# First stage of a decoder-layer kernel: modulation slabs and sample query strips issued earlier, weight sums moved on VectorE

## The chip, the core and the metric

The program runs on one core of one Trainium2 chip. Its time is the device time of one execution in microseconds, as a median of several runs. The engines are TensorE (PE in the profile, its weight loads PEld), VectorE (DVE), ScalarE (ACT), GpSimd (POOL) and SyncE (SP); each runs its own list of instructions in order, and they wait for one another with counting semaphores. SP and ACT issue the DMA transfers, each on a queue of its own (q1 carries what SP issues, q10 what ACT issues).

## The reference, cut to what matters

One layer for 1024 prompt rows and 8 sample rows (one new token each, with 4096 cached positions in pages of 128). All in float32:

```python
shift, scale, gate = split(silu(c) @ w_ada + b_ada, 3)
h = rmsnorm(x, g_pre) * (1 + scale) + shift
hc, bc, cc, gc, q, k, v, ga = split(h @ w_in, 8)      # 512 columns each
u = cc * hc
ya = rmsnorm(bc * conv3(u), g_conv) * silu(gc)
o = stick_breaking_attention(q, k, v, b_sb)            # sample rows: over the paged cache
yb = rmsnorm(o, g_attn) * silu(ga)
y = x + gate * rmsnorm(concat(ya, yb) @ w_out, g_post)
```

## The kernel before

The kernel has a first stage, then four groups g of two heads and 128 conv channels (SLOTS = 32 slots t of each group), then the output projection. The order on each engine is written out by hand, so every engine's function lists its own steps.

**First stage.** x is scaled and turned into hT (eight slices k of 128 channels, by 1056 columns). `ada(n)` (line 1508) multiplies silu(c) with slab n of w_ada: shift and scale of the lower half of the channels are slabs 0 and 1, of the upper half 2 and 3. ACT copies each result (`ada_copy`, 755), `mod_sums(a)` (1538) adds up its four strips, and DVE's `modulation(a)` (1109), `modulate_samples(a)` (1120) and `modulate(a, c)` (1126) scale and shift the half a of hT, counting up h_ready. `project_qk(m, a)` (1545) is a sixth of group 0's Q and K projection for half a; the halves a = 1 close the sums, and ACT takes them out in `evac_qk` (788).

**Sample queries.** `strips(DB, ..., 4)` (1592) projects the sample rows to all heads' queries; ACT copies them to qsP (769), `query_rows` (1558) adds the strips, ACT copies the rows (771), writes them to q_rows in DRAM (773), waits until that has landed (774) and reads two of them back into qb, broadcast over the partitions (776). GpSimd's page products (673) can start only then: each multiplies one pair of K pages with qb, and DVE's `reduce_pair` (1337) sums each. There are two `prod` buffers, so product p waits for reduction p - 2. SP loads the K pages into a ring of four pairs (474).

**Gates.** `gate_strips(n)` (1513) projects slabs 4 and 5 of w_ada (numbered 5 and 7 as loads), ACT copies them (`gate_strips`, 778), `gate_sums(n)` (1521) adds them on PE, and DVE's `gates(n)` (1151) makes gps and gp in four dependent steps. `gate_strips(1)` waits for three steps of `gates(0)`.

**Group 0's block products.** A projection pair is made with Strassen-like products `product(g, i, j)` (1760): chunk i, product j of seven. Chunks 2 and 3 of group 0 are V and B. Products 3, 5 and 6 read sums of weights, which for V and B DVE makes in four steps (`value_weight_sum`, 1182), with S1 lying in the same tile as qsP; product 7 reads the fourth. `product(0, 2, 4)`, code 24, waits at line 1797 for d_c22, which DVE's `product_sum(.., 2, 7)` (1207, 1227) counts. That sum stands in slot t = 6 of DVE's list, behind the reductions of page pairs 0 to 9 (slots 1 to 5) and before `gates(1)`. EARLY_FIRST (101) is PE's order of codes in slots 6 and 7 of group 0, TAKEN_FIRST (103) ACT's order of taking them out.

**Loads.** `load_w` (783) on ACT loads 512 KB of w_in in rows of 512 bytes. In slot 0 of group 0, V and B are loaded when qk_full reaches 1 (792, 793). SP loads slab 5 of w_ada (line 476) after four K page pairs and once ada_ps has reached 5.

Of the kernel before, what the change touches and what calls it, by code (L numbers as in the profile page):

```python
# [27 lines left out]
ALU = mybir.AluOpType  # L28
# [4 lines left out]
D = 1024  # L33
KT = D // P
SEQ = 1024
TT = SEQ // P
NB = 8
NT = SEQ + NB
NTP = SEQ + 32
# [9 lines left out]
EPS = 1e-6  # L49
# [94 lines left out]
def stick_breaking_mixer(nc, x_prompt, x_sample, c_prompt, c_sample, cache_k, cache_v, state_conv,  # L144
# [4 lines left out]
    with ctx:  # L149
# [564 lines left out]
        def _(act):  # L714
# [52 lines left out]
            ada_copy(3)  # L767
            act.wait_ge(qs_ps, 1)
            run(qsP, ps[:, DB, :], ACT.Copy, qs_copied, scale=HD ** -0.5)
            act.wait_ge(qs_ps, 2)  # L770
            run(qsP[0:NB, :], ps[0:NB, DB, :], ACT.Copy, qs_copied)
            act.wait_ge(qs_copied, 2)
# [15 lines left out]
            def evac_qk(g, m):  # L788

                act.wait_ge(qk_full, m + 1)  # L790
                if m == 0:
                    load_w(g, V_, 2)
                    load_w(g, BC_, 3)
                if m == 2:
                    load_w(g, GC_, 0)
                if m == 5:
                    load_w(g, GA_, 1)
                src = ps[:, QK_BANK[m], :]
                if m < 3:
                    n = CH if m < 2 else SEQ - 2 * CH  # L800
                    run(qT[:, CH * m:CH * m + n], src[:, 0:n], ACT.Copy, qk_free, scale=HD ** -0.5)
                else:
                    run(kT[:, CH * (m - 3):CH * (m - 2)], src[:, 0:CH], ACT.Copy, qk_free)
# [140 lines left out]
            def body(g, first, last):  # L944
                for t in range(SLOTS + 1):
                    u = t - 8
                    if 0 <= u < NU:
                        lo, head = first_col(u), UNITS[u][3]
                        act.wait_ge(zc_ready, NU * g + u + 1)
                        if not (first and u < 2):  # L950
                            act.wait_ge(lw_ready, NU * g + u - 1)
                        run(rise[:, u % 2, lo:QC], ps[:, Z + u % 3, 0:QC - lo], ACT.Relu, rise_ready,
                            bias=bsh[:, bass.ds(2 * g + head, 1)])
                        z = sp[:, lo:QC]
                        if not (first and u < 1):
                            act.wait_ge(ln_done, NU * g + u)
                        run(z, zc[:, u % 3, lo:QC], ACT.Exp, exp_done)
                        act.wait_ge(exp_done, NU * g + u + 1)
                        run(ps[:, Z + u % 3, 0:QC - lo], z, ACT.Ln, ln_done, bias=1.0)
                    if u >= 1:  # L960
                        weights(g, u - 1, first)
                    if first and t < 6:
                        evac_qk(g, t)
                    for code in (TAKEN_FIRST if first else TAKEN).get(t, ()):
                        evac_st(g, code // 10, code % 10)
                    if t in (4, 6) and not first:
                        squares(g - 1, t // 6)
                        if t == 4:
                            sample_columns(g - 1)
                    if t == 7:  # L970
                        value_rows_copy(g, first, 0)
                        key_rows_copy(g, 0, first)
                    if t == 9:
                        value_rows_copy(g, first, 1)
                    if t == 8:
                        key_rows_copy(g, 1, first)
                    if t == 19:
                        out_copy(g)
                    if t >= 8 and t < SLOTS and u % 2 == 1:
                        i = u // 2  # L980
                        for back, j in {0: ((-1, 4), (0, 1)), 1: ((0, 5), (0, 2), (0, 6)), 2: ()}[i % 3]:
                            evac_st(g, 4 + i // 3 + back, j)
                    if first and t in (1, 5):
                        gate_strips(t // 5)
                    if t == 10:
                        key_rows_copy(g, 2, first)
                    if t in (21, 27):
                        silu_step(g, t // 27, 0)
                    if t in (22, 28):
                        silu_step(g, t // 28, 1)  # L990
                    if t in (23, 29):
                        silu_step(g, t // 29, 2)
                    if t in (25, 31):
                        silu_end(g, t // 31)
                    if t == 11:
                        decode_logs(g, 0)
                    if t == 19:
                        decode_a(g, 0, first)

                evac_st(g, CHUNKS - 1, 4)  # L1000
                for j in () if last else AHEAD[:2]:
                    evac_st(g + 1, 0, j)
                decode_logs(g, 1)
                for j in () if last else AHEAD[2:]:
                    evac_st(g + 1, 0, j)
                decode_a(g, 1, first)
# [37 lines left out]
        def _(v):  # L1044
# [51 lines left out]
            for k in range(KT):  # L1096
                v.wait_ge(xT_full, k + 1)
                v.tensor_copy(hT[:, k, 0:HALF], ps[:, k % 4, :]).then_inc(xT_dve, 1)
            v.wait_ge(ssq, TT + 1)
            v.tensor_scalar(ss[:, 4:TT], ss[:, 4:TT], 1.0 / D, EPS, ALU.mult, ALU.add).then_inc(var_ready, 1)  # L1100
            v.tensor_scalar(ss[0:NB, TT:TT + 1], ss[0:NB, TT:TT + 1], 1.0 / D, EPS, ALU.mult, ALU.add)\
                .then_inc(var_ready, 1)
            v.wait_ge(rstd_ready, 3)
            row_scales(4)
            v.tensor_scalar(xs, xs, rs[0:NB, TT:TT + 1], None, ALU.mult).then_inc(x_scaled, 1)
# [123 lines left out]
            def body(g, first, last):  # L1229
# [18 lines left out]
                for t in range(SLOTS):  # L1248
                    u = t - 8
                    if u >= 1:  # L1250
                        log_weights(g, u - 1, first)
                    if t == 18 and g == 2:
                        own_heads(0)
                    if t == 20 and g == 2:
                        own_heads_copy(0)
                    chunk = (SUMMED_FIRST if first else SUMMED).get(t)
                    if u > 0 and u % 6 == 0:
                        chunk = 3 + u // 6
                    if chunk is not None:
                        product_sum(g, first, chunk, 3)  # L1260
                        product_sum(g, first, chunk, 7)
                    if first and t == 6:
                        gates(1)
                    if u >= 0 and u % 2 == 0:
                        clamp(g, u, first)
                        clamp(g, u + 1, first)
                    if t == 14:
                        decode_log_weights(0)
                    for p in sums_at(t):
                        reduce_pair(g, p)  # L1270
                    if t in (2, 3):
                        value_weight_sum(g, 2 * (t - 2))
                        value_weight_sum(g, 2 * (t - 2) + 1)
                    if not first and t in GATING_AT:
                        gating(g - 1, GATING_AT[t])
                    if first and t == 0:
                        channel_sums()
                    if first and t == 0:
                        gates(0)

                log_weights(g, NU - 1, first)
# [197 lines left out]
        def _(pe):  # L1479
# [99 lines left out]
            pe.wait_ge(xT_act, 5)  # L1579
            project_qk(0, 0)  # L1580
            ada(2)
            pe.wait_ge(xT_act, 6)
            project_qk(1, 0)
            ada(3)
            pe.wait_ge(xT_act, 7)
            project_qk(2, 0)
            mod_sums(1)
            pe.wait_ge(ada_copied, 4)
            project_qk(3, 0)
            project_qk(4, 0)  # L1590
            pe.wait_ge(h_ready, 14)
            strips(DB, lambda k: hT[:, k, SEQ:NTP], 4).then_inc(qs_ps, 1)
            project_qk(5, 0)
            query_rows()
            project_qk(0, 1)
            gate_strips(0)
            project_qk(1, 1)
# [1 line left out]
            gate_sums(0)  # L1599
            for m in range(3, 6):  # L1600
                project_qk(m, 1)
            gate_strips(1)

            def body(g, first, last_):
                def value_rows(c):
# [91 lines left out]
                for t in range(8):  # L1697
                    if first and t == 6:
                        pe.wait_ge(qk_free, 6)
                        mm(ps[:, BY, 0:SC], ident[:, :], hT[:, 0, 0:SC], True, True)  # L1700
                    for at, code in enumerate(EARLY_FIRST.get(t, ()) if first else EARLY[t]):
                        product(g, code // 10, code % 10)
                        if first and t == 6 and at == 0:
                            gate_sums(1)
                    if t == 7:
                        value_rows(0)
                        key_rows(0)
                        product(g, 4, 1)
                    page_values(t)
# [235 lines left out]
```

## Time and profile before

| what | us |
|---|---|
| median of 3 runs | 810.47 |
| lowest, highest run | 808.97, 810.64 |
| the profiled execution, its own time | 807.52 |
| span in its profile | 805.8 |
| PE busy in the span | 766.9 |
| DVE, POOL, ACT busy | 567.1, 433.1, 360.7 |

The span goes from the first instruction to the last, so 1.7 us of the profiled execution's time lie outside it. A timeline row is: start, duration, engine, line, operation, what is written and read, shape, count, and in brackets the idle time before it with what ended it. Line 1481 is the helper through which every matmul goes; a float32 matmul shows as two records.

### The profile page before, as it was taken

The numbers are of one execution on the slowest core, as the hardware profiler recorded it, in microseconds if no ns is written. First come the engines' busy times: TensorE is split into PE (matmuls) and PEld (weight loads), VectorE is DVE, ScalarE is ACT, GpSimd is POOL, SyncE is SP. The second block draws the span as 40 slices with busy tenths as digits, with TensorE's granted clock in tenths as the row PEclk, the third lists the DMA queues.
The fourth block names the chain that finished last, engine by engine and source line by source line (L and its number), as shares of the span: only waits on it lengthen the run. The fifth ranks groups of instructions, "written<-read, shape, count | busy, mean of one in ns | idle before, by whom it ended". The sixth has DMA issues, their size and how long they took to land.

```text
span 805.8 us, 13959 instructions
## 1 busy us (share of the span) xinstructions
PE 766.9 (95%) x4113; PEld 510.0 (63%) x4113; DVE 567.1 (70%) x743; ACT 360.7 (45%) x769; POOL 433.1 (54%) x231
## 2 busy tenths in 40 slices
PE   1898899999999999999999999999999999999995
PEld 1654586767787667668876767787667654343432
DVE  4656768888698688777968788798588766232344
ACT  6311127678312657761136678312657752212122
POOL 1004876676777756868784775877757650100000
PEclk9999999999999999999999999999999999999999
DMA  8979738587788889778899878799987898654001
GB/s 314 372 278 309 251 103 269 180 269 249 248 269 287 279 254 301 248 223 266 296 288 291 267 254 248 240 282 300 281 267 239 281 344 342 205 183 136 28 27 55
DMA packets 131118, 197.83 MB, mean 246 GB/s; under 512 B 10073, under 2 KB 51078, under 8 KB 131042
## 3 DMA queue, kind: packets, MB, share of 16 engines
q1 hardware_dynamic: 99256, 180.57, 67.3%
q10 hardware_dynamic: 31786, 16.36, 7.5%
q8 instruction: 33, 0.54, 0.3%
q14 instruction: 43, 0.35, 0.1%
HBM read 185.25 MB, written 11.66 MB: 244 GB/s over the span
## 4 chain that ended last, share of the span: by engine, by line
PE 80%; DVE 7%; SPq 3%; issue 3%; DMA 3%; POOL 2%; ACT 1%; POOLq 0%; DVEq 0%; ACTq 0%
PE ps L1481 74%; PE ps L1657 3%; DMA rise<-in_w_out_dram 1%; POOL prod L673 1%; SPq L432 1%; DVE zd L1341 1%; PE ps L1534 1%; SPq L424 1%; DMA xT<-in_x_prompt_dram 1%; DVE ps L1365 1%; DVE xT L1086 1%; SPq L438 0%; DVE zc L1351 0%; PE ps L1616 0%; PE ps L1689 0%
## 5 line engine op out<-in xcount | busy, mean ns | idle before, releaser
L673 POOL TENSOR_TENSOR prod<-ring,qb 128x1024 f32<-128x1024 f32 x128 | 313.8, 2465 | 203.4 <-DVE zd L1341 84.0
L1341 DVE TENSOR_REDUCE zd<-prod 128x16 f32<-128x1024 f32 x128 | 154.0, 1211 | 19.2 <-POOL prod L673 19.0
L1481 PE MATMUL ps<-hT,wsl 128*128 128x258 f32 (+1 forms) x576 | 146.2, 396 | 0.3 <-DVE zb L1246 0.2
L1481 PEld LDWEIGHTS ps<-hT,wsl 128*128 128x128 f32 x576 | 107.1, 190 | 33.2 <-issue 12.7
L1481 PE MATMUL ps<-xT,wsl 128*128 128x258 f32 x480 | 121.4, 388 | 4.0 <-DVE bcb L1227 4.0
L1481 PE MATMUL ps<-xT,wS 128*128 128x258 f32 x480 | 124.1, 388 | 0.0
L1481 PEld LDWEIGHTS ps<-xT,wsl 128*128 128x128 f32 x480 | 87.0, 190 | 30.2 <-issue 10.8
L1481 PEld LDWEIGHTS ps<-xT,wS 128*128 128x128 f32 x480 | 87.3, 192 | 20.4 <-issue 10.1
L1365 DVE TENSOR_TENSOR_SCAN ps<-rise,ps 128x512 f32<-128x512 f32 (+3 forms) x64 | 65.5, 1023 | 34.5 <-ACT ps L716 34.2
L1481 PE MATMUL ps<-ring,apad 128*32 128x512 f32 (+3 forms) x592 | 80.5, 622 | 2.6 <-DMA ring<-in_w_ada_dram 2.6
L716 ACT ACTIVATE av<-ps 128x512 f32<-128x512 f32 (+4 forms) x104 | 49.9, 480 | 70.6 <-PE ps L1657 57.3
L716 ACT ACTIVATE rise<-ps,bsh 128x512 f32<-128x512 f32 (+3 forms) x96 | 55.4, 577 | 51.7 <-DVE zc L1351 51.6
L1351 DVE TENSOR_SCALAR zc<-ps,bsb 128x512 f32<-128x512 f32 (+3 forms) x96 | 54.7, 612 | 27.9 <-PE ps L1481 27.6
L1481 PE MATMUL ps<-hT,wS 128*128 128x258 f32 x240 | 62.3, 391 | 0.0
L1481 PEld LDWEIGHTS ps<-hT,wS 128*128 128x128 f32 x240 | 42.5, 190 | 19.0 <-issue 14.6
L1371 DVE TENSOR_TENSOR zc<-zc,ps 128x512 f32<-128x512 f32 (+3 forms) x96 | 52.8, 550 | 2.2
L709 POOL TENSOR_TENSOR rs<-ss,half 128x1 f32<-128x1 f32 x8 | 4.3, 544 | 89.6 <-DVE ss L1463 89.6
L1657 PE MATMUL ps<-ident,zc 128*128 128x128 f32 x288 | 47.6, 274 | 2.6 <-DVE zc L1371 2.6
L716 ACT ACTIVATE sp<-zc 128x512 f32<-128x512 f32 (+3 forms) x96 | 49.7, 517 | 0.0
L716 ACT ACTIVATE ps<-sp 128x512 f32<-128x512 f32 (+3 forms) x96 | 47.5, 495 | 3.0
L1481 PEld LDWEIGHTS ps<-av,vN 128*64 128x64 f32 x576 | 30.5, 136 | 27.5 <-issue 25.7
L1657 PEld LDWEIGHTS ps<-ident,zc 128*128 128x128 f32 x288 | 36.0, 141 | 14.5 <-DVE zc L1371 6.6
(259 smaller groups left out, 991.2 us busy)
## 6 DMA issues: line engine op xcount, KB each, us to landing
ring<-in_cache_k_dram SPq DMA_DIRECT2D x256, 256.0 KB, 3.8
ring<-in_cache_v_dram SPq DMA_DIRECT2D x256, 256.0 KB, 3.0
wsl<-in_w_in_dram ACTq DMA_DIRECT2D x30, 512.0 KB, 6.7
ring<-in_w_ada_dram SPq DMA_DIRECT2D x5, 2048.0 KB, 15.0
xT<-in_x_prompt_dram SPq DMA_DIRECT2D x2, 2048.0 KB, 11.2
out_dram<-oT SPq DMA_DIRECT2D x8, 512.0 KB, 4.6
xT<-in_x_prompt_dram SPq DMA_DIRECT2D x6, 512.0 KB, 8.1
ring<-in_w_in_dram SPq DMA_DIRECT2D x1, 2048.0 KB, 17.0
```

Of the source, the lines that this page charges most:

```text
L424: _, numbers = nc.values_load_multi_w_load_instructions(pages[0:1, bass.ds(seq * PAGES + (PAGES - 2 - r), 2)], engines=[mybir.EngineType.S ...
L432: sp_e.dma_start(dst[:, j, :], src).then_inc(full, 16)
L673: pool.tensor_tensor(prod[:, p % 2].rearrange("p (j c) -> p j c", j=2), kring[:, p % 4], qb[:, p // 16].unsqueeze(1).to_broadcast([P, 2, H ...
L716: nc.scalar.activation(out, in_, func, **kw).then_inc(done, 1)
L1086: v.tensor_scalar(xy[:, t, :], xy[:, t, :], rs[:, t:t + 1], None, ALU.mult).then_inc(x_scaled, 1)
L1341: v.tensor_reduce(zd[:, t // 16, :, r:r + 2], prod[:, t % 2].rearrange("p (j h d) -> p h j d", j=2, h=NH), AX_X, ALU.add)\
L1351: v.tensor_scalar(zc[:, u % 3, lo:QC], ps[:, Z + u % 3, 0:QC - lo], bsb[:, bass.ds(2 * g + h, 1)], CLAMP, ALU.add, ALU.min).then_inc(zc_re ...
L1365: v.tensor_tensor_scan(back(sums), back(rise[:, par_, lo + 1:QC + 1]), back(sums), start, ALU.add, ALU.add).then_inc(scan_done, 1)
L1371: v.tensor_tensor(zc[:, u % 3, lo:QC], zc[:, u % 3, lo:QC], sums, ALU.subtract)\
L1481: return nc.tensor.matmul(out, l, r, start=start, stop=stop, skip_group_check=True)
L1534: last = nc.tensor.transpose(ps[:, k % 4, P * j:P * (j + 1)], xy[:, 4 * h + j, P * k:P * (k + 1)], ident[:, :])
L1657: last = nc.tensor.transpose(ps[:, Z + u % 3, P * j:P * (j + 1)], zc[:, u % 3, lo + P * j:lo + P * (j + 1)], ident[:, :])
```

## The change

PE: `ada(3)` goes ahead of `project_qk(1, 0)`, `mod_sums(1)` ahead of `project_qk(2, 0)`; the sample strips go ahead of `project_qk(3, 0)`, and `query_rows` right behind it. `gate_strips(1)` leaves the end of the first stage for slot 6, behind the third product there; `gate_sums(1)` goes from behind the first to behind the fourth. ACT: the loads of V and B are issued right after the first copy of the sample queries, and the copy of `gate_strips(1)` goes from slot 5 to slot 6. DVE: the variances of x's second half are made after four of the eight copies of hT in place of after all eight; the four weight sums of V and B go from slots 2 and 3 to slot 0, between `channel_sums` and `gates(0)`, for group 0.

```diff
@@ ACT
             run(qsP, ps[:, DB, :], ACT.Copy, qs_copied, scale=HD ** -0.5)
+            for slot, part in ((2, V_), (3, BC_)):
+                act.dma_start(wsl[:, slot, :, :], w_v[PART[part]][0]).then_inc(w_full[slot], 16)
             act.wait_ge(qs_ps, 2)
...
                 act.wait_ge(qk_full, m + 1)
-                if m == 0:
-                    load_w(g, V_, 2)
-                    load_w(g, BC_, 3)
...
-                    for code in (TAKEN_FIRST if first else TAKEN).get(t, ()):
+                    for at, code in enumerate((TAKEN_FIRST if first else TAKEN).get(t, ())):
                         evac_st(g, code // 10, code % 10)
+                        if first and t == 6 and at == 2:
+                            gate_strips(1)
...
-                    if first and t in (1, 5):
-                        gate_strips(t // 5)
+                    if first and t == 1:
+                        gate_strips(0)
@@ DVE
             for k in range(KT):
                 v.wait_ge(xT_full, k + 1)
                 v.tensor_copy(hT[:, k, 0:HALF], ps[:, k % 4, :]).then_inc(xT_dve, 1)
-            v.wait_ge(ssq, TT + 1)
-            v.tensor_scalar(ss[:, 4:TT], ss[:, 4:TT], 1.0 / D, EPS, ALU.mult, ALU.add).then_inc(var_ready, 1)
...
+                if k == 3:
+                    v.wait_ge(ssq, TT + 1)
+                    v.tensor_scalar(ss[:, 4:TT], ss[:, 4:TT], 1.0 / D, EPS, ALU.mult, ALU.add).then_inc(var_ready, 1)
...
-                    if t in (2, 3):
+                    if not first and t in (2, 3):
                         value_weight_sum(g, 2 * (t - 2))
                         value_weight_sum(g, 2 * (t - 2) + 1)
...
                     if first and t == 0:
                         channel_sums()
-                    if first and t == 0:
+                        for step in range(4):
+                            value_weight_sum(g, step)
                         gates(0)
@@ PE
             project_qk(0, 0)
             ada(2)
+            ada(3)
             pe.wait_ge(xT_act, 6)
             project_qk(1, 0)
-            ada(3)
+            mod_sums(1)
             pe.wait_ge(xT_act, 7)
             project_qk(2, 0)
-            mod_sums(1)
+            pe.wait_ge(h_ready, 14)
+            strips(DB, lambda k: hT[:, k, SEQ:NTP], 4).then_inc(qs_ps, 1)
             pe.wait_ge(ada_copied, 4)
             project_qk(3, 0)
+            query_rows()
             project_qk(4, 0)
-            pe.wait_ge(h_ready, 14)
-            strips(DB, lambda k: hT[:, k, SEQ:NTP], 4).then_inc(qs_ps, 1)
             project_qk(5, 0)
-            query_rows()
...
-            gate_strips(1)
...
-                        if first and t == 6 and at == 0:
+                        if first and t == 6 and at == 2:
+                            gate_strips(1)
+                        if first and t == 6 and at == 3:
                             gate_sums(1)
```

## Rows read from the trace of the kernel before

**Rows 1.** The page: the chain that ended last, by engine.
```profile
PE 80%; DVE 7%; SPq 3%; issue 3%; DMA 3%; POOL 2%; ACT 1%; POOLq 0%; DVEq 0%; ACTq 0%
```

**Rows 2.** PE's waits in the whole span: total us, times, longest.
```profile
PE ps L1481 <- DVE bcb L1227: 4.0, 1, 4.0
...
PE ps L1657 <- DVE zc L1371: 2.6, 5, 0.9
```

**Rows 3.** PE's timeline, 37 to 110 us: start, us, what, [idle before].
```profile
43.93 1.93 PE L1481 MATMUL ps<-ring,apad 128*32 128x512 f32 x16
...
49.90 4.87 PE L1481 MATMUL ps<-hT,wsl 128*128 128x344 f32 x16
54.70 1.93 PE L1481 MATMUL ps<-ring,hT 128*32 128x512 f32 x16
...
69.21 2.08 PE L1481 MATMUL ps<-ssa,e 128*8 128x512 f32 x4
...
80.49 1.92 PE L1481 MATMUL ps<-ring,apad 128*32 128x512 f32 x16 [2.26 <-DMA ring<-in_w_ada_dram]
...
95.34 1.90 PE L1481 MATMUL ps<-hT,wsl 128*128 128x258 f32 x8
101.28 2.53 PE L1481 MATMUL ps<-xT,wsl 128*128 128x258 f32 x8 [4.03 <-DVE bcb L1227]
103.60 3.11 PE L1481 MATMUL ps<-xT,wS 128*128 128x258 f32 x8
```

**Rows 4.** Stretches: us, busy (x) of PE, PEld, DVE, ACT, POOL, PEclk, DMA, GB/s.
```profile
104.00:106.00 2.00, 2.00 (x6) 1.59 (x5) 1.84 (x3) 0.60 (x2) 0.00 (x0) 0.50 0.26 98
```

**Rows 5.** DVE's timeline, 62 to 101 us.
```profile
62.70 2.31 DVE L1180 TENSOR_TENSOR xT<-hT,xT 128x2064 f32<-128x2064 f32 x1
70.35 0.68 DVE L1158 TENSOR_TENSOR rows<-ps,ub 8x512 f32<-8x512 f32 x1 [5.33 <-PE ps L1481]
71.06 2.49 DVE L1160 TENSOR_TENSOR rows<-rows,gab 8x512 f32<-8x512 f32 x1
...
74.92 2.34 DVE L1341 TENSOR_REDUCE zd<-prod 128x16 f32<-128x1024 f32 x2
...
82.10 0.69 DVE L1192 TENSOR_TENSOR wS<-wsl 128x512 f32<-128x512 f32 x1
...
90.55 2.83 DVE L1205 TENSOR_TENSOR wsl<-wsl 128x512 f32<-128x512 f32 x1
...
100.81 0.42 DVE L1227 TENSOR_TENSOR bcb<-ps,stage 128x258 f32<-128x258 f32 x1
```

**Rows 6.** POOL's timeline, 68 to 95 us.
```profile
68.35 4.66 POOL L673 TENSOR_TENSOR prod<-ring,qb 128x1024 f32<-128x1024 f32 x2 [40.89 <-DMA qb<-q_rows]
...
82.29 10.54 POOL L673 TENSOR_TENSOR prod<-ring,qb 128x1024 f32<-128x1024 f32 x4 [1.36 <-DMA ring<-in_cache_k_dram]
```

**Rows 7.** ACT's timeline, 60 to 80 us, with its DMA issues.
```profile
60.75 0.28 ACTq L773 DMA_DIRECT2D q_rows<-wS  x1
63.20 0.85 ACTq L776 DMA_DIRECT2D qb<-q_rows  x2
...
79.01 0.46 ACT L716 ACTIVATE kT<-ps 128x344 f32<-128x344 f32 x1 [2.60 <-PE ps L1481]
```

**Rows 8.** SP's timeline, 58 to 66 us.
```profile
58.21 7.15 SPq L432 DMA_DIRECT2D ring<-in_cache_k_dram  x8
```

**Rows 9.** DMA issues, KB, us to landing: slab 3 (issued 29.07), B (issued 64.5).
```profile
ring<-in_w_ada_dram SPq DMA_DIRECT2D x1, 2048.0 KB, 11.4
wsl<-in_w_in_dram ACTq DMA_DIRECT2D x1, 512.0 KB, 17.5
```

**Rows 10.** Queues (packets, MB, share of 16 engines): SP's at 60.7:64, ACT's at 70:76, 110:113.
```profile
q1 hardware_dynamic: 395, 0.71, 66.6%
q10 hardware_dynamic: 1076, 0.54, 32.5%
q10 hardware_dynamic: 1040, 0.52, 58.6%
```

More of the change, by code:

```diff
@@ L1098, in _ @@
                 v.tensor_copy(hT[:, k, 0:HALF], ps[:, k % 4, :]).then_inc(xT_dve, 1)
-            v.wait_ge(ssq, TT + 1)
-            v.tensor_scalar(ss[:, 4:TT], ss[:, 4:TT], 1.0 / D, EPS, ALU.mult, ALU.add).then_inc(var_ready, 1)
-            v.tensor_scalar(ss[0:NB, TT:TT + 1], ss[0:NB, TT:TT + 1], 1.0 / D, EPS, ALU.mult, ALU.add)\
-                .then_inc(var_ready, 1)
+                if k == 3:
+                    v.wait_ge(ssq, TT + 1)
+                    v.tensor_scalar(ss[:, 4:TT], ss[:, 4:TT], 1.0 / D, EPS, ALU.mult, ALU.add).then_inc(var_ready, 1)
+                    v.tensor_scalar(ss[0:NB, TT:TT + 1], ss[0:NB, TT:TT + 1], 1.0 / D, EPS, ALU.mult, ALU.add)\
+                        .then_inc(var_ready, 1)
             v.wait_ge(rstd_ready, 3)
```

## Prediction

> **What bounds the kernel now.** Read the chain that ended last first: PE holds 80% of it [rows 1]. Then PE's waits over the span [rows 2]: the longest behind the opening loads is 4.0 us for one DVE result, while its transposes in the attention slots wait 2.6 us in five waits. So behind 110 us PE is nearly always busy, and time taken from PE's list in the first stage comes off the end, unless POOL or DVE can't follow. PE's timeline [rows 3] shows two holes that this change can reach. One ends at 80.49 (2.26 us, slab 5 of w_ada). The other runs from 97.25 to 101.28 (4.03 us) ahead of product 24, and the next two products take 2.32 and 2.95 us, start to start, where others take 1.74: the granted clock at 104 to 106 is 0.50, the 1.2 GHz level [rows 4]. Those 1.8 us are the second hole's follow-up cost.
>
> What ends the second hole is read on DVE and POOL. Product 24 waits for product_sum(2, 7), whose record ends at 101.23 [rows 5]; it stands behind ten reductions, each behind a page product of POOL. POOL starts at 68.35 when qb lands; products 0 and 1 are done at 73.0, but DVE reduces them from 74.92, behind gates(0) [rows 5, 6]. Then K pair 4 comes late (1.36 us) and four page products take 10.54 us, 2.63 each for 2.33, while DVE's weight sums take up to 2.83 us each for 0.69 [rows 5, 6].
>
> **The change part by part.**
>
> *PE up to slot 6* issues the same matmuls in another order; up to 78.23 (where the hole before 80.49 begins) it has no wait before, and I look for new ones. ada(3) would start one chunk product earlier, 43.93 - 2.5 = 41.4; its slab landed at 29.07 + 11.4 = 40.5 [rows 3, 9]. No wait, with 0.9 us to spare. mod_sums(1) comes one chunk product (4.87 / 2 = 2.4 us) earlier, and with it modulation(1), modulate and channel_sums; the last of these, ending at 65.0 before, ends at 62.6 [rows 3, 5]. The sample strips start at 49.9 in place of 54.70, query_rows ends near 55.1 in place of 60.0, and q_rows is issued at 60.75 - 4.9 = 55.9 [rows 3, 7]. Slab 4, which the strips need, came behind slab 3 on SP's queue; at 48 us it has landed if the queue went on at the same pace. The moved variances only start the second half's rsqrt up to 1.9 us earlier; I count 0, since that half's row scaling still stands behind the copies in DVE's list. It is worth up to 1 us if POOL's share there (1.6 us) is hidden; the PE wait for it ended in the chain before 37 us, so the bound is 0 to +1.
>
> *The first hole.* gate_strips(1) covered it no longer: PE's next wait is for ACT's copy of the last K chunk, 79.01 + 0.46, so it restarts near 79.55: hole 1.3, gain 0.95 [rows 3, 7]. gate_strips(1) moves three products on; SP issues its slab once gate_strips(0) is done (64.4, before 65.4 because of the K loads [rows 8]) and needs it at 85.4; 15 us of load as before would do.
>
> *PE in slot 6.* From 79.55: 0.54 opening, 1.83 for product 21, six of 1.74, 1.86 for the gate strips, 1.92 for gate_sums(1), and 0.1 of drain: product 24 is reached at 96.3 (97.25 before, the 0.95 again).
>
> *V and B loads and DVE's sums.* They leave slots 2 and 3, so the reductions meet no DVE operation that shares time with POOL. Unchanged stands gates(0), bound by gate_sums(0) on PE at 69.21 [rows 3]: reductions start at 74.9 as before. Then POOL's product 2 starts at 76.27 and product 9 ends 8 x 2.33 later, 94.9; reduction 9 ends at 96.15, and the record of product_sum(2, 7) 0.75 behind it, 96.9. K pair 4 must have landed at 80.9; it is issued near 71 behind slab 5, which now has no V and B beside it: yes. Product 24 would start at 96.95, a hole of 0.6.
> The condition is when qb lands (T). ACT's queue now has V and B (1 MB) ahead of q_rows, and SP's K loads start 4.8 us earlier, beside them. I bound it by queue shares [rows 10]: with SP's K loads at 66.6% of the engines, a third is left; at 32.5% ACT's queue moved 0.54 MB in 6 us (90 GB/s), at 58.6% 0.52 MB in 3 (173). From 52.6 to the end of the K issues at 53.4 + 7.15 = 60.6 [rows 8] that is 0.7 MB, the rest 1 to 2 us more: V and B land near 63, q_out comes at 63 to 65.5, qb 5 to 6.3 us later: T = 68.5 to 71.5 against 68.35. DVE's four sums wait for q_out and take 2.8 us: done by 68.3, before gates(0) can begin at 70.35. ACT, waiting for q_out, holds evac_qk(0) and the copy of gate_strips(0); PE's gate_sums(0) needs that at 69.2, with 2.4 us of ACT work before it, so q_out may come by 66.8 for nothing. T up to 71.6 lets both products end by 76.3. But POOL's products then lie on gates(0), one step of which took 2.49 us beside POOL against 0.68 [rows 5]; with T near 69.5 its last step is held too. I take 0.5 us for that (bounds 0 and 1.3): product 24 starts at 97.4.
>
> The Trainium skill (DMA: Bandwidth & Descriptors, section on queues, rings and completion order) says that each DMA engine takes turns between queues packet by packet and a ring's descriptors in order. By it q_rows can't pass V and B: this speaks against the change and is the rival "queue" below. The trace agrees so far as B, issued beside SP's large loads, took 17.5 us to land [rows 9].
>
> *The clock.* With the hole at 1.1 us the two products behind it should take 1.74: the hole of 2.26 us at 80.49 was followed by no slower one in rows 3 (82.89 to 97.24 are eight steps of 1.74 to 1.9). Gain 2.32 + 2.95 - 2 x 1.74 = 1.8. The bound is 0, if it falls anyway.
> The Trainium skill (TensorE: Matmul & The Clock Gate, Part 1) says that the throttled level is the default, which activity releases and idleness brings back; a shorter hole then keeps 2.4 GHz. By the other reading, that the fall was not the hole's, this term is nothing and the gain 3.9.
>
> *Behind it.* DVE's part shifts by 3.9 and PE's by 5.7. DVE had 1.3 and 2.7 us idle between the products' sums and the first clamp (110 to 117 us), which takes up the 1.8. In the later groups nothing is changed. The loads at the end are released by the compute and shift with it.
>
> **Sum.** 101.28 - 97.4 = 3.9, plus 1.8: 5.7 us. Against the profiled execution, 807.5 - 5.7 = 801.8; that execution is 2.95 us below the median of the runs shown, so the time forecast is 810.5 - 5.7 = 804.8.
>
> **The rivals.**
> *Queue (slower).* V and B land as slowly as B did before, 17.5 us: 52.9 + 17.5 = 70.4, q_out 71. PE stalls at gate_sums(0) by 4.2 us, gates(0) is as late, qb lands at 77.5, POOL's product 2 starts at 82.2 in place of 76.3, product 24 at 102.9 and the clock falls as before: 1.6 us slower, 812.1. It decides from T = 75.9. For it: one queue, small rows, K loads moved beside them. Against: SP's queue was idle from 54 to 58 us and the K loads left a third free, whereas B had slab 5 (2 MB) queued against it.
> *Half way.* T near 73 to 75: product 24 at 98.5 to 100.5, clock falls or not: gain 1 to 4, middle 2.5, 808.
> *Clock.* The hole goes, the slow products stay, or come elsewhere: gain 3.9, 806.6.
> *Ahead.* qb lands before 66.4, or DVE's gates slip past POOL: the reductions start 1.8 us earlier and PE finds product 24 free at 96.3: gain 4.95 + 1.8 = 6.7, 803.8; with the moved variances up to 7.7, 802.8.
>
> **How the numbers follow.** Forecast 0.50 (its own range 803.5 to 806.1), clock 0.15, half way 0.13, queue 0.12, ahead 0.10. Measurement tells about 0.2% (1.6 us) from no change. Faster takes the forecast, clock, ahead and half of half way: 0.81. Same takes the rest of half way and a little of queue: 0.09. Slower: 0.10. The range runs from 802.6 to 809.4: it reaches from ahead to most of half way and leaves out queue.
>
> **What would show it.** In the changed kernel's trace: ada(3) without a wait near 41.4; q_rows issued near 56 and POOL's first product at 68.5 to 71.5; weight sums of 0.69 us before gates(0); the hole after the K chunks 1.3 us; POOL's ten products without a DMA wait, 2.33 us each; product 24 near 97.4 and PEclk 1.00 behind it. The forecast is wrong if q_out comes after 67 (a wait of PE at gate_sums(0)), or if PE waits for slab 3 or 4, or if the 5.7 us at 110 us come back as waits for zc later.

## Result, and the profile after

The changed kernel took 801.04 us as the median of 4 runs (800.35 to 802.22), the kernel before 810.56 (4 runs): a ratio of 0.9895, 95% interval 0.9869 to 0.9922, so faster by 6.3 to 10.6 us, about 1%. Two later jobs repeated the comparison: 0.9919 (0.9894 to 0.9943) and 0.9910 (0.9886 to 0.9935). Taken together over the four jobs, 55 runs of before have a median of 808.86 us (805.57 to 813.67) and 16 of the changed kernel 801.78 (799.13 to 804.07): 7.1 us. I had forecast a gain of 5.7 us and a time of 804.8, in a range from 802.6 to 809.4. The sign was right and the size too small.

The span of the profiled execution is 799.9 us against 805.8. PE's timeline of the changed kernel from 28 to 106 us (columns as in [rows 3]):

```profile
28.86 1.97 PE L1537 MATMUL ps<-ident,xT 128*128 128x128 f32 x16
...
40.62 1.92 PE L1484 MATMUL ps<-ring,apad 128*32 128x512 f32 x16 [1.21 <-DMA ring<-in_w_ada_dram]
...
49.09 1.92 PE L1484 MATMUL ps<-ring,hT 128*32 128x512 f32 x16
...
68.22 2.08 PE L1484 MATMUL ps<-ssa,e 128*8 128x512 f32 x4
...
78.55 0.70 PE L1484 MATMUL ps<-hT,ident 128*128 128x258 f32 x2 [1.30 <-ACT kT L716]
...
95.33 1.90 PE L1484 MATMUL ps<-xT,wsl 128*128 128x258 f32 x8
97.07 1.90 PE L1484 MATMUL ps<-xT,wS 128*128 128x258 f32 x8
...
105.77 0.60 PE L1618 MATMUL ps<-ident,av 128*128 128x128 f32 x4
```

The row at 95.33 is product 24. It stood at 101.28 [rows 3]; it has no idle time in front of it now, and the one behind it starts 1.74 us later. I use the last row, the first transpose of the value rows, as a mark: everything that the change moves on PE lies ahead of it. It stood at 113.51 us in the trace of before, so PE is 7.74 us ahead there.

DVE of the changed kernel, 63 to 95 us, and POOL's page products:

```profile
63.36 0.69 DVE L1194 TENSOR_TENSOR wS<-wsl 128x512 f32<-128x512 f32 x1 [1.64 <-DMA wsl<-in_w_in_dram]
...
70.07 1.17 DVE L1162 TENSOR_TENSOR rows<-rows,gab 8x512 f32<-8x512 f32 x1
...
72.61 2.34 DVE L1344 TENSOR_REDUCE zd<-prod 128x16 f32<-128x1024 f32 x2
...
94.02 0.42 DVE L1229 TENSOR_TENSOR bcb<-ps,stage 128x258 f32<-128x258 f32 x1
```

```profile
65.84 4.86 POOL L673 TENSOR_TENSOR prod<-ring,qb 128x1024 f32<-128x1024 f32 x2 [41.18 <-DMA qb<-q_rows]
73.97 23.17 POOL L673 TENSOR_TENSOR prod<-ring,qb 128x1024 f32<-128x1024 f32 x10 [3.27 <-DVE zd L1344]
```

Against [rows 5, 6]: the first reduction starts 2.3 us earlier (1.3 us of it from the second step of gates(0), 1.17 us in place of 2.49, and 1.0 because PE's gate_sums(0) starts at 68.22 in place of 69.21), POOL's products run 2.32 us each without a break, and the sum that frees product 24 ends at 94.44 in place of 101.23. ACT's queue (start, length, issue) gives the times of q_rows: issued at 55.13, landed when qb is issued at 60.46, where before it took from 60.75 to 63.20 [rows 7].

```profile
51.09 1.03 ACTq L771 DMA_DIRECT2D wsl<-in_w_in_dram  x2
...
55.13 0.30 ACTq L775 DMA_DIRECT2D q_rows<-wS  x1
60.46 0.85 ACTq L778 DMA_DIRECT2D qb<-q_rows  x2
```

**From the mark to the end.** The span is 5.9 us shorter, not 7.7. I split each trace at two rows, the mark and the first of the final sums over ssa:

| profile | mark | sums over ssa | span | mark to sums | sums to end |
|---|---|---|---|---|---|
| before | 113.51 | 682.13 | 805.8 | 568.62 | 123.7 |
| changed | 105.77 | 674.59 | 799.9 | 568.82 | 125.3 |
| changed, second profile | 105.73 | 673.75 | 797.4 | 568.02 | 123.7 |
| changed, third profile | 105.66 | 675.72 | 801.0 | 570.06 | 125.3 |

The mark is the same to 0.1 us in all three profiles of the changed kernel. What lies behind it differs by up to 2 us in the middle and takes one of two lengths at the end. In the first profile of the changed kernel the granted clock (last but two) is down longer there:

```profile
678.00:680.00 2.00, 2.00 (x14) 1.30 (x17) 0.17 (x1) 0.00 (x0) 0.51 (x1) 0.50 0.00 0
680.00:682.00 2.00, 2.00 (x16) 0.21 (x8) 0.00 (x0) 0.00 (x0) 2.00 (x1) 0.50 0.00 0
682.00:684.00 2.00, 2.00 (x6) 0.84 (x3) 0.00 (x0) 0.00 (x0) 0.41 (x1) 0.50 0.78 251
684.00:686.00 2.00, 2.00 (x5) 0.76 (x4) 0.00 (x0) 0.57 (x1) 0.00 (x0) 0.97 0.70 202
```

In the second profile of the changed kernel, same place, it is down for less time:

```profile
677.00:679.00 2.00, 2.00 (x17) 0.83 (x20) 0.17 (x1) 0.00 (x0) 1.16 (x1) 0.79 0.00 0
679.00:681.00 2.00, 2.00 (x9) 0.50 (x2) 0.00 (x0) 0.00 (x0) 1.76 (x1) 0.50 0.59 135
681.00:683.00 2.00, 2.00 (x5) 0.89 (x4) 0.00 (x0) 0.02 (x1) 0.00 (x0) 0.86 0.71 203
```

That belongs to the execution and not to the kernel: both lengths occur in the same kernel, and all 14 profiles of this case have a last part of either 123.6 to 123.7 or 125.2 to 125.3 us. So single spans are good to some 3 us, and the mark tells the value of an edit in the first stage far better.

### The profile page after: what moved, and what is told of

It is laid out like the page before. It is cut to its first block, busy times and chain, and to the rows that moved or that the text cites. A ratio compares the mean times of both kernels' runs of the same rounds, so it can differ in the third digit from the quotient of the medians.

```text
span 799.9 us, 13959 instructions
## 1 busy us (share of the span) xinstructions
PE 765.4 (96%) x4113; PEld 508.2 (64%) x4113; DVE 560.7 (70%) x743; ACT 361.1 (45%) x769; POOL 431.7 (54%) x231
## 3 DMA queue, kind: packets, MB, share of 16 engines
q1 hardware_dynamic: 99256, 180.57, 68.5%
## 4 chain that ended last, share of the span: by engine, by line
PE 82%; DMA 6%; DVE 5%; SPq 3%; issue 2%; ACT 1%; POOLq 0%; POOL 0%; ACTq 0%; DVEq 0%
PE ps L1484 77%; DMA ring<-in_w_ada_dram 4%; PE ps L1659 3%; DMA rise<-in_w_out_dram 2%; SPq L432 1%; SPq L424 1%; DVE ps L1368 1%; DVE zd L1344 1%; DVE zc L1354 0%; PE ps L1691 0%; PE ps L1618 0%; SPq L438 0%; DVE zc L1374 0%; DVE ps L1244 0%; SPq L442 0%
## 5 line engine op out<-in xcount | busy, mean ns | idle before, releaser
L1484 PEld LDWEIGHTS ps<-xT,wsl 128*128 128x128 f32 x480 | 86.9, 190 | 25.7 <-issue 10.8
L1368 DVE TENSOR_TENSOR_SCAN ps<-rise,ps 128x512 f32<-128x512 f32 (+3 forms) x64 | 65.5, 1024 | 34.0 <-ACT ps L716 33.8
L1484 PEld LDWEIGHTS ps<-av,vN 128*64 128x64 f32 x576 | 30.5, 136 | 27.5 <-issue 25.7
```

The lines of the kernel that those rows point to most:

```text
L1368: v.tensor_tensor_scan(back(sums), back(rise[:, par_, lo + 1:QC + 1]), back(sums), start, ALU.add, ALU.add).then_inc(scan_done, 1)
L1484: return nc.tensor.matmul(out, l, r, start=start, stop=stop, skip_group_check=True)
```

## Experiments

**The changed kernel again, in two more jobs.** No edit.

> The changed kernel once more, as the scale for the others of this job. Theory A (the first stage alone gives the gain): PE reaches the transposes of the value rows near 105.8 us as in the first profile, 7.7 us ahead of before, and the median is 7 to 8.5 us below before's. Theory B (the profile's 5.9 us are the gain and the 9.5 us of the runs an accident): median 5 to 6.5 us below.

Measured: 802.61 us median of 6 (before 808.94), mark 105.73.

> The changed kernel a third time, for the size of the gain in the runs. Reading of the traces: 7.7 us at the value rows' transposes, and a tail (from the sums over ssa to the end) of either 123.65 or 125.3 us by where the clock falls: median 6 to 9 us below before's. If the first job's 9.5 us were the gain, it is again over 9; if the second's 6.5 us, again under 7.

Measured: 801.69 us median of 6 (before 808.63), mark 105.66. Differences of 6.3 and 6.9 us. The 6.3 lie in the range of theory B and the mark at that of theory A, which a median of six runs doesn't decide. Neither the first job's 9.5 nor the first profile's 5.9 is the gain. Seven us are, and 7.7, the lead at the mark, lies within the interval of each of the three comparisons.

**The moved variances, alone and undone.** In the first kernel this is the only edit to before; in the second it is the only part of the change that is undone.

```diff
             for k in range(KT):
                 v.wait_ge(xT_full, k + 1)
                 v.tensor_copy(hT[:, k, 0:HALF], ps[:, k % 4, :]).then_inc(xT_dve, 1)
-            v.wait_ge(ssq, TT + 1)
...
+                if k == 3:
+                    v.wait_ge(ssq, TT + 1)
...
```

> Before with one part of the change alone: the variances of x's second half made after four of the eight copies of hT. Theory A (this part is worth what PE waited for DVE's row scaling): the second half's transposes on PE start at 28.9 in place of 30.94, slab 3 is needed at 41.9 and has landed at 40.5, and the transposes of the value rows start at 111.4 in place of 113.5: 2.1 us faster. Theory B (my prediction's count of nothing): 30.9, 113.5, same time.

> The changed kernel with the variances put back behind all eight copies. Theory A (2.1 us gained on PE, 1.2 lost again to slab 3): no PE wait for slab 3, the value rows' transposes start at 106.7 in place of 105.8, 0.9 us slower than the changed kernel, 6.8 us ahead of before. Rival (variances worth nothing): 105.8. Rival (2.1 us whole): 107.9.

Measured alone: the second half's transposes at 29.02 and the mark at 111.25, 2.26 us ahead of before; 807.51 us, ratio 0.9990 (0.9968 to 1.0013), so the runs don't separate it from before, and don't exclude 2.3 us either. Theory A holds for this kernel. Undone: mark at 106.01, 0.24 us behind the changed kernel and nearer to the rival "worth nothing" (105.8) than to theory A (106.7); 801.30 us, ratio 0.9910, the same as with it. PE's timeline of the kernel with the variances put back:

```profile
30.54 1.97 PE L1536 MATMUL ps<-ident,xT 128*128 128x128 f32 x16 [1.93 <-DVE bcb L1106]
...
40.89 1.90 PE L1483 MATMUL ps<-ring,apad 128*32 128x512 f32 x16
```

The edit takes away this wait, 30.54 to 28.86, and ada(3), which needs slab 3 at 40.6, gives 1.2 us of it back. Those two parts of the change are in each other's way: ada(3) was moved ahead to where its slab has just landed without the variances, and not yet with them.

**A hole ahead of product 24.** The order of two steps on DVE is exchanged in the changed kernel:

```diff
-                    if chunk is not None:
-                        product_sum(g, first, chunk, 3)
-                        product_sum(g, first, chunk, 7)
                     if first and t == 6:
                         gates(1)
+                    if chunk is not None:
+                        product_sum(g, first, chunk, 3)
+                        product_sum(g, first, chunk, 7)
```

> The changed kernel with gates(1) ahead of product_sum(2) on DVE, which makes product 24 on PE wait. Both theories: a hole of about 5 us ahead of product 24 (start near 100.4 in place of 95.33). Theory A (the slow clock follows the hole): PEclk near 0.50 some us behind it, the next two products take 2.3 to 3 us in place of 1.74, and the value rows' transposes start near 112.6, 6.9 us later than in the changed kernel. Theory B (the slow products had another cause, as V's and B's weight sums or the loads at that time): PEclk stays 1.00, two products of 1.74, and 110.9.

Measured: mark 112.98, 807.10 us (10 runs). PE's timeline:

```profile
99.66 3.81 PE L1484 MATMUL ps<-xT,wsl 128*128 128x258 f32 x8 [4.03 <-DVE bcb L1229]
103.26 2.92 PE L1484 MATMUL ps<-xT,wS 128*128 128x258 f32 x8
106.02 1.90 PE L1484 MATMUL ps<-hT,wsl 128*128 128x258 f32 x8
```

A hole of the length of [rows 3], without weight sums or late loads beside it, brings the slow clock: the two products take 3.60 and 2.76 us in place of 1.74 each. Theory A stands. The follow-up cost is 2.9 us here, 1.8 in before.

**V and B loaded late, or behind q_rows.** Both take the loads away from behind the first copy of qsP. The first puts them back into evac_qk(0), the second behind the issue of q_rows.

```diff
+                if m == 0:
+                    load_w(g, V_, 2)
+                    load_w(g, BC_, 3)
```

```diff
             act.dma_start(q_rows, qsP[0:NB, :]).then_inc(q_out, 16)
+            for slot, part in ((2, V_), (3, BC_)):
+                act.dma_start(wsl[:, slot, :, :], w_v[PART[part]][0]).then_inc(w_full[slot], 16)
             act.wait_ge(q_out, 16)
```

> The changed kernel with the loads of V and B put back to where evac_qk(0) issues them, the sums staying in slot 0. If the early loads are what carries the sums' new place: B lands near 79.5 (17.5 us behind its issue, as in before), the four sums end near 82.3 and gates(0) behind them, the reductions start near 85 in place of 72.6, product 24 near 106 to 107, the clock falls, the value rows' transposes start near 118 to 119 in place of 105.8. If the sums could do with late loads: within 1 us of 105.8. The second q_rows question: without V and B ahead of it, q_out should come 2.4 us behind its issue (57.5) in place of 5.3.

> The changed kernel with V's and B's loads issued behind q_rows on ACT's queue, not ahead of it. Theory A (V and B ahead delay q_rows on its queue): q_out 2.4 us behind the issue in place of 5.3. Theory B (the engines are loaded by SP's K loads, the order on ACT's queue does nothing): near 5. The price is then at the other end: qb is read behind V and B, POOL's first product near 67 to 69, B lands near 66 and the sums end by 69; the transposes of the value rows start within 1 us of 105.8.

Measured, late: q_out 2.7 us behind its issue (55.05 to 57.73). B landed 7.3 us behind its own issue, at 69.3, and did not take 17.5. The mark is at 107.21, product 24 at 96.66 with a hole of 1.26 us and no slow clock; one run, 802.42 us. DVE's timeline:

```profile
69.30 0.69 DVE L1195 TENSOR_TENSOR wS<-wsl 128x512 f32<-128x512 f32 x1 [7.66 <-DMA wsl<-in_w_in_dram]
...
74.79 2.34 DVE L1345 TENSOR_REDUCE zd<-prod 128x16 f32<-128x1024 f32 x2
```

So the early loads are worth 1.4 us, not the 13 I expected of them. This run also prices the chain behind the reductions: started at 74.79, near the 74.9 of my forecast, they make a hole of 1.26 us ahead of product 24. Measured, behind q_rows: q_out 1.8 us behind its issue (55.20 to 57.00), qb landed at 65.2 all the same (8.2 us in place of 5.5), mark 105.98, one run, 799.85 us. The two sums that then fell beside POOL's first products took 2.78 and 2.82 us, and PE didn't wait for them. Having V and B ahead costs q_rows some 3 us on its queue, and it gets them back in front of qb.

**The weight sums back in slots 2 and 3.**

```diff
-                    if not first and t in (2, 3):
+                    if t in (2, 3):
...
-                        for step in range(4):
-                            value_weight_sum(g, step)
```

> The changed kernel with V's and B's weight sums back in DVE's slots 2 and 3, between the reductions. Theory (the reductions and POOL's products are stretched by sums that share time with POOL): sums of 1.7 to 2.8 us each, product_sum(2) near 96.8 in place of 93.7, product 24 near 97.5 with a hole of 2.2 us, transposes of the value rows at 108 with the clock kept and 109.8 without. Rival (the gain came from the loads alone): product 24 at 95.3, transposes at 105.8.

Measured: 806.89 us (10 runs), ratio to before 0.9973 (0.9952 to 0.9994); mark 109.19, 3.4 us behind the changed kernel. Its DVE and PE:

```profile
79.36 1.69 DVE L1194 TENSOR_TENSOR wS<-wsl 128x512 f32<-128x512 f32 x1
81.15 2.65 DVE L1200 TENSOR_TENSOR wS<-wS,wsl 128x512 f32<-128x512 f32 x1
...
85.98 2.02 DVE L1205 TENSOR_TENSOR wS<-wsl,wS 128x512 f32<-128x512 f32 x1
87.92 2.83 DVE L1207 TENSOR_TENSOR wsl<-wsl 128x512 f32<-128x512 f32 x1
```

```profile
98.65 2.01 PE L1482 MATMUL ps<-xT,wsl 128*128 128x258 f32 x8 [2.71 <-DVE bcb L1229]
100.49 1.90 PE L1482 MATMUL ps<-xT,wS 128*128 128x258 f32 x8
```

9.2 us of DVE time beside POOL for 2.8 alone. Of the parts that were undone one by one, this placement is the largest: 3.4 us at the mark with the clock kept. The order on PE up to slot 6 and the move of `gate_strips(1)` were not undone alone. The runs put the kernel 5 us behind the changed one's 801.8, more than its one profile does; a slow clock behind the 2.71 us hole in some executions would account for it, but no profile here shows that.

**Looking for a faster version.** Four edits; (a) and (d) were also run alone, (b) and (c) only with others. (a) is another order on PE, (b) GA's load issued behind the last K chunk's copy, (c) `gate_strips(1)` back at the end of the first stage, and (d) the four steps of gates(0) one by one in DVE's slots 1 to 4. (a), waits left out, and (d):

```diff
             ada(2)
-            ada(3)
             project_qk(1, 0)
-            mod_sums(1)
+            ada(3)
             project_qk(2, 0)
-            strips(DB, lambda k: hT[:, k, SEQ:NTP], 4).then_inc(qs_ps, 1)
+            mod_sums(1)
             project_qk(3, 0)
-            query_rows()
+            strips(DB, lambda k: hT[:, k, SEQ:NTP], 4).then_inc(qs_ps, 1)
             project_qk(4, 0)
+            query_rows()
```

```diff
-                        gates(0)
+                    if first and 1 <= t <= 4:
+                        gates(0, (t - 1,))
```

> The changed kernel with three edits: ada(3) behind project_qk(1, 0) and mod_sums(1) behind project_qk(2, 0) again, with the sample strips behind project_qk(3, 0) (slab 3 has landed by then: minus 1.2 us); gate_strips(1) back at the end of the first stage (its slab landed at 72.4, PE is there at 76: covers the hole of 1.3 us); GA's load issued behind the last K chunk's copy (minus 0.7 of that hole). Expected: PE reaches product 24 at 92.8, DVE gives it at 93.3 to 94.0, transposes of the value rows near 103.8 to 104.4, 1.4 to 2 us ahead of the changed kernel. Rival: POOL's products now fall on gates(0) (qb lands 1.2 us later) and product 24 stays at 95.3: no gain.

> The changed kernel with ada(3) behind project_qk(1, 0), mod_sums(1) behind project_qk(2, 0) and the sample strips behind project_qk(3, 0). PE no longer waits 1.2 us for slab 3, so PE is at gate_sums(0) at 67.0 as in best1; but qb lands near 66 and POOL's products fall on gates(0) (its second step 2.3 us in place of 1.2), so the reductions start near 72.5 as before and product 24 starts near 94.6, with a hole of about 0.5 us: value rows' transposes near 105.0, 0.7 us gained of the 1.2.

> The changed kernel with the four steps of gates(0) spread over DVE's slots 1 to 4, behind the reductions of each, in place of all four ahead of the first reduction. If gates(0) is what holds POOL's third product (73.97, 3.3 us of idle POOL): POOL goes on without a hole from 65.8, product 9 ends near 90, product_sum(2) comes as soon as PE's product 27 is done, near 93.2 in place of 94.0; product 24 starts at 95.3 all the same (PE was not waiting), transposes 105.8.

> The spread steps of gates(0), the order of after_ada3 and GA's load behind the last K chunk's copy, together. PE reaches product 24 at 93.4 (1.2 us from slab 3, 0.7 from the copy) and DVE has it ready by 92 to 93: no hole, no fall of the clock, transposes of the value rows near 103.8, 1.95 us ahead of the changed kernel; median 1 to 3 us below the changed kernel's, if the tail's clock falls alike. Rival: a K pair or gate step 3 comes late and the gain is under 0.5 us.

Measured: best1 (a, b, c) 801.79 us, ratio 0.9914, mark 106.88, 1.1 us behind the changed kernel: PE was ready at 92.7 but DVE gave product 24 at 94.6, as the rival on record had it in the main, and the clock fell behind the hole. after_ada3 (a alone) mark 104.50, one run at 798.3. after_spread (d alone) mark 105.92: POOL's twelve products ran from 65.86 in one piece, and PE got nothing of it, as expected. best4 (a, b, d) mark 104.55, 800.04 us, ratio 0.9909 (0.9878 to 0.9941): a wait of 0.83 us for the third gate step takes the place of what (b) gave. Its PE:

```profile
76.43 0.70 PE L1489 MATMUL ps<-hT,ident 128*128 128x258 f32 x2 [0.55 <-ACT kT L716]
...
83.18 1.93 PE L1489 MATMUL ps<-ring,apad 128*32 128x512 f32 x16 [0.83 <-DVE ub L1168]
```

The order (a) alone shows 1.2 to 1.3 us at the mark; the runs tell neither version from the changed kernel. PE's timeline of best1, for the clock:

```profile
94.64 3.07 PE L1482 MATMUL ps<-xT,wsl 128*128 128x258 f32 x8 [1.93 <-DVE bcb L1227]
97.50 2.57 PE L1482 MATMUL ps<-xT,wS 128*128 128x258 f32 x8
```

## Why the prediction was right and where it was wrong

**The mechanism** was right: both holes, the chain of POOL and DVE behind the second, the weight sums beside POOL and the clock's follow-up cost were the terms, and the changed kernel has 5.95 us less at product 24 and 1.79 more behind it (I had 3.9 and 1.8). The first hole came out at 1.30 us as forecast, and the clock's 1.8 to 0.01 us.

**Product 24** started at 95.33, not 97.4. Of these 2.07 us, PE reached it 0.97 earlier than I had (96.3): the second half's transposes started 2.08 us earlier (28.86 against 30.94), the wait for slab 3 took 1.21 of them back, and 0.1 came from steps that follow each other more closely. The other 1.1 are the hole that I had left ahead of it, and that is the step that failed: the time T at which qb lands, with the load on gates(0) that I had drawn from it (2.49 us for its second step and 0.5 more). Of the 2.3 us by which the reductions came earlier, this is 1.3; the other 1.0 is PE's earlier gate_sums(0), which I had left unchanged.

**T.** I let q_out come when V and B have landed, at 63 to 65.5, and qb at 68.5 to 71.5. q_out came at 60.4, and qb at 65.8, earlier even than in before, so POOL's two products were mostly over when gates(0) began, its second step took 1.17 us and not 2.49, and the reductions started at 72.6. The mis-sized term is the share of the engines that V and B get beside SP's K loads. I had given them the third that the K loads leave where these run alone [rows 10], which is 0.7 MB from 52.6 to 60.6. The queues of the changed kernel from 52.6 to 58 us:

```profile
q10 hardware_dynamic: 1865, 0.94, 66.7%
q1 hardware_dynamic: 435, 0.83, 43.6%
```

The K loads gave way, and their issue rows took 8.05 us in place of 7.15 [rows 8]. ACT's queue moved 0.94 MB in 5.4 us, 174 GB/s in place of 90, so most of V and B was over by 58. The three profiles of the changed kernel show what repeats. V landed at 58.8, 58.1 and 57.5, B at 63.3, 61.0 and 60.5, and q_out came at 60.5, 60.4 and 60.5. In the first, q_rows passed B by 2.9 us, while in the other two it landed within 0.6 us of B; either way it came 2.5 us or more ahead of my range. That q_rows can't pass V and B was too strong a reading of the Trainium skill (DMA: Bandwidth & Descriptors, queues, rings and completion order): the same section also says that completion isn't first in, first out for an issuing engine. The first profile agrees with that: 16 KB issued 3.6 us behind B landed 2.9 us ahead of it. But the earlier q_out doesn't rest on it, since it came as early where B had all but landed.

**The variances** I counted at 0 with a bound of 1, because the row scaling stands behind the copies in DVE's list. But in before the copies were over by 25.7, and DVE then waited 1.63 us for POOL's powers, which waited for the variances. In the changed kernel the scaling starts at 25.38 without a wait, 2.12 us earlier. PE's transposes came 1.7 us earlier for it (against the kernel with this part undone), and at the mark 0.24 us was left. That kernel's opening happened to run 0.4 us ahead of before's (30.54 against 30.94), so up to 0.6 is possible. The 0 nearly holds in the sum, by another wait (slab 3) that I had not joined to it. I had given ada(3) 0.9 us to spare from the order before; with the variances moved it was 1.2 us short.

**The rival "queue"** had the price of B's load wrong: it took 17.5 us in before, where the K loads, qb and slab 5 fell on the same stretch, and 7.3 when issued late in the changed kernel, where the K loads and qb were out of the way. Which of them had made the 17.5 was not taken apart. The rival "ahead" described what happened (qb before 66.4, no hole, gain 6.7, 7.7 with the variances, 802.8) and I had given it 0.10. Its condition was two microseconds from my range for T, on the one duration that I had not bounded below: the time of V, B and q_rows on ACT's queue beside the K loads.

**The clock.** I took the 2.26 us hole without a slow product as showing that short holes cost nothing. The runs show otherwise (below). The term was right here by luck: because the hole vanished altogether.

**Median and range.** The time forecast was 810.5 - 5.7. The three runs shown were a high draw: 808.86 is the median of 55 later and earlier runs. With the mark's 7.7 us, the trace accounts for 808.9 - 7.7 = 801.2. Of the 3.8 us between 804.8 and 801.04, 2.0 are the terms above; the other 1.7 go with the level of before, which was itself 2.95 us above the profiled execution that the sum was made against. My range gave no room for that spread, though both numbers stood in the table.

## To carry to other kernels

Price an edit at the last row that it can move, not at the span: here the mark repeats to 0.1 us where spans differ by 3.6 and medians by 1.6. Put DVE work that POOL's products stretch where POOL is idle: the four sums cost 2.8 us there and 9.2 between page products. When two parts of a change each bring PE forward, lay them on one timeline before giving either a margin: the second may use up the slack of the first. And a queue's share where it runs alone is no bound for what is left to another beside it: 66.6% became 43.6%.

## What the runs showed of the hardware

The length of a hole alone did not decide whether the clock fell to its 1.2 GHz level. Holes of 4.03 us (before, and the exchanged order) were followed by it. Of the shorter ones, 1.93 (best1), 1.96 (after_spread, at 26.95) and 2.14 and 2.18 us (before with the variances moved, at 78.45 and 99.02) were; but 1.94 (before, at 30.94), 1.93 (variances put back, at 30.54), 2.26 (before, at 80.49) and 2.71 (sums in slots 2 and 3) were not. The one of 2.14, in stretches of PE's granted clock:

```profile
78.00:80.00 2.00, 1.55 (x12) 0.68 (x16) 1.31 (x2) 0.00 (x0) 0.66 (x1) 0.70 1.09 358
80.00:82.00 2.00, 2.00 (x12) 0.34 (x5) 1.90 (x2) 0.17 (x1) 1.75 (x1) 0.50 1.10 350
```

None of the holes of 1.15 to 1.74 us was followed by it. What else decides was not settled. A 512 KB load of w_in in 512-byte rows took 4.5 to 17.5 us to land in the first 112 us of before, with other transfers in flight beside it each time; what set the length was not taken apart.
